# Decoder block on one core: the first two phases merged, half of a later weight product moved into them, and expert rows scattered to a table by token and choice

## What is computed

```python
mod = jax.nn.silu(c) @ w_ada[l] + b_ada[l]                       # 1024 x 6144 weights, one row of 6144
sh_m, sc_m, gt_m, sh_f, sc_f, gt_f = jnp.split(mod, 6, axis=-1)
h = modulate(rmsnorm(x, g_norm_mix[l]), sh_m, sc_m)              # needs the first 2048 columns of mod
z = h @ w_in[l]                                                  # RWKV columns, latent (MLA) columns, gates
...                                                              # RWKV scan, group norm, attention, branches
x = x + gt_m[:, None, :] * (merged @ w_out[l])
h2 = modulate(rmsnorm(x, g_norm_ffn[l]), sh_f, sc_f)             # needs columns 3072 to 5120 of mod
x = x + gt_f[:, None, :] * hier_moe(h2, ...)                     # 32 experts, 2 of them for each token
```

## Time and profile before

| | us |
|---|---|
| median of 3 runs | 1671.89 |
| lowest and highest of them | 1671.5, 1673.9 |
| profiled execution, device time | 1669.98 |
| its span | 1668.2 |
| PE busy in the span | 1427.4 (86%) |
| DMA engines busy, queue q1 (issued by SP) | 35.4% |

### The profile page before, as it was taken

The page is one execution under the profiler, slowest core; times in us unless marked ns, Lnnn a source line. Parts: engine busy times, 40 slices in busy tenths (PEclk is TensorE's granted clock), DMA queues, the critical chain, the costliest instruction groups (busy, mean ns, idle before and its releaser), DMA issues. The chain is left out here.

```text
span 1668.2 us, 32819 instructions
## 1 busy us (share of the span) xinstructions
PE 1427.4 (86%) x14321; PEld 1024.3 (61%) x14321; DVE 704.3 (42%) x991; ACT 464.2 (28%) x827; POOL 249.0 (15%) x292
## 2 busy tenths in 40 slices
PE   7499999847999984499988999999896699999980
PEld 3497777627999981277767888787785333333320
DVE  1545677566666636144444111355335221111114
ACT  0543223252434322144434222212111111111110
POOL 0001122105656520011110000000000100000003
PEclk9699999978999997699998999999997699999995
DMA  6711222100000009990002111314106789999957
GB/s 256 251 56 51 83 81 83 58 15 2 5 4 4 4 8 318 313 371 1 1 1 76 50 50 50 139 51 152 42 39 260 265 326 420 421 421 401 410 212 302
DMA packets 76582, 252.35 MB, mean 151 GB/s; under 512 B 7128, under 2 KB 32216, under 8 KB 59680
## 3 DMA queue, kind: packets, MB, share of 16 engines
q1 hardware_dynamic: 66800, 220.48, 35.4%
q0 software_dynamic: 6048, 16.79, 2.8%
q10 hardware_dynamic: 3600, 13.11, 1.9%
HBM read 211.00 MB, written 44.58 MB: 153 GB/s over the span
## 5 line engine op out<-in xcount | busy, mean ns | idle before, releaser
L2418 PE MATMUL ps<-gu,xT 128*32 128x512 f32 x1536 | 178.3, 606 | 4.6 <-DMA gu<-w_e_up 3.9
L394 PE MATMUL ps<-hs,wh 128*128 128x512 f32 x320 | 126.7, 396 | 11.5 <-DVE hs L390 7.9
L396 PE MATMUL ps<-hs,wl 128*128 128x512 f32 x320 | 126.5, 395 | 0.0
L2418 PEld LDWEIGHTS ps<-gu,xT 128*32 128x32 f32 x1536 | 48.2, 112 | 111.6 <-issue 107.6
L2640 DVE TENSOR_TENSOR sg<-sg,ps 128x256 f32<-128x256 f32 x25 | 10.5, 422 | 217.3 <-ACT sg L2504 217.3
L395 PE MATMUL ps<-hs,wh 128*128 128x512 f32 x256 | 100.6, 393 | 0.0
L390 DVE TENSOR_TENSOR wl<-wraw,wh 128x1024 fp32r<-128x1024 f32 x24 | 29.4, 1225 | 156.2 <-ACT wh L387 156.2
L394 PE MATMUL ps<-hh,wr_h 128*128 128x512 f32 x224 | 93.1, 416 | 0.6 <-DVE wr_l L390 0.6
L395 PE MATMUL ps<-hl,wr_h 128*128 128x512 f32 x224 | 88.4, 395 | 0.0
L396 PE MATMUL ps<-hh,wr_l 128*128 128x512 f32 x224 | 88.4, 395 | 0.0
L1895 DVE TENSOR_REDUCE nmax<-ps 128x1 f32<-128x896 f32 (+4 forms) x64 | 45.9, 754 | 99.9 <-PE ps L1804 99.4
(11 more groups left out here) (358 smaller groups left out, 3037.0 us busy)
## 6 DMA issues: line engine op xcount, KB each, us to landing
gu<-w_e_gate SPq DMA_DIRECT2D x34, 1024.0 KB, 13.8
gu<-w_e_up SPq DMA_DIRECT2D x34, 1024.0 KB, 16.3
dn<-w_e_down SPq DMA_DIRECT2D x34, 1024.0 KB, 12.6
wada<-w_ada SPq DMA_DIRECT2D x16, 1024.0 KB, 6.7
expert_rows<-YTM ACTq DMA_DIRECT2D x25, 512.0 KB, 8.8
wbuf<-w_ada SPq DMA_DIRECT2D x4, 2048.0 KB, 15.5
wraw<-w_gates SPq DMA_DIRECT2D x16, 512.0 KB, 3.4
expert_rows<-zrow SPq DMA_DIRECT2D x4, 2048.0 KB, 24.6
```

What stands on the lines that cost most here:

```text
L394: nc.tensor.matmul(out, wt[0], mov[0], start=(k == 0), stop=False)
L396: return nc.tensor.matmul(out, wt[1], mov[0], start=False, stop=(k == kn - 1))
L2418: last = nc.tensor.matmul(ps[part, GB[b]], xT[:, b, k, part], gu[:, expert(m, c_) % WB, :, k], start=(k == 0), stop=(k == KD - 1))
```

## The change

1. **Front.** Phase 0 is gone; its work is in phase 1. The first 2048 columns are now a `Rows` object too (`rows0`): 8 pieces of 1 MB in 8 slots, with the tiles of x loaded between them, products in four column groups. DVE adds the bias and the gain in a layout of 4 x 32 partitions, and four products with a selection matrix (`sel`) bring the rows to all 128 partitions; ACT copies `SH_M` and DVE `SC_M` out of PSUM.
2. **`rows4` moved to the front** as 16 half pieces (256 of each 512 columns, 512 KB, in runs of 1 KB) in three slots. PE makes two half pieces after the transposes of each tile. Its row is stored at the end of the front's list. `wm_l` is now made by POOL.
3. **Phase 4** keeps `rows2` alone, with 6 slots; SP issues `pair(0)` first and the other pairs right behind the pieces.
4. **Expert rows.** The table `expert_rows` has 2048 rows, one for each choice and token. POOL scatters the result rows there by indirect DMA (indices `home`), five passes behind its fetches; rows without a token are left out. The zeros are no longer written. In the last phase SP loads 16 tiles of 128 rows with plain DMAs.

```diff
+            def load(self, sp, i):
+                if i >= self.room:
+                    sp.wait_ge(self.mm, i - self.room + 1)
+                at = slice(i // KD * self.width, (i // KD + 1) * self.width)
...
+                    for k in range(KD):
+                        rows0.load(sp, k)
+                        if k % 2:
+                            load_x(k // 2)
...
+                    for t in range(NT):
+                        if t + 4 < NT:
+                            sp.wait_ge(h_ready, t + 1)
+                            load_x(t + 4)
+                        for i in range(NW + 2 * t, min(NW + 2 * t + 2, rows4.pieces)):
+                            rows4.load(sp, i)
+                        if t:
+                            store(t - 1)
...
+                    pool.wait_ge(wm_hi, 1)
+                    nc.gpsimd.tensor_tensor(wm_l[:], wm[:], wm_h[:].bitcast(f32), ALU.subtract).then_inc(wm_lo, 1)
...
-                            if t == 1:
-                                dve.wait_ge(wm_hi, 1)
-                                low_part(wm_l[:], wm[:], wm_h[:]).then_inc(wm_lo, 1)
...
+                    roots(0)
+                    rows0.add_bias(dve, CH + 2)
+                    dve.wait_ge(rows0.done, 1)
+                    nc.vector.scalar_tensor_tensor(row0[64:P], row0[64:P], 1.0, gains[64:P], ALU.add, ALU.mult)\
+                      .then_inc(rows0.done, 1)
+                    dve.wait_ge(bc_mm, 1)
+                    link(nc.vector.tensor_copy(SC_M, ps[:, 2:4].rearrange("p a n -> p (a n)")))
...
+                    for j in range(CH):
+                        m = nc.tensor.matmul(ps[:, j], sel[:, j], row0, start=True, stop=True)
+                    m.then_inc(bc_mm, 1)
...
+                        for i in range(2 * t, 2 * t + 2):
+                            rows4.products(pe, i)
                         if t >= 2:
                             mla(t - 2)
...
+                    pair(0)
                     for k in range(KD):
                         rows2.load(sp, k)
-                    pair(0)
-                    for k in range(KD):
-                        rows4.load(sp, k)
-                    rows2.store(sp, 1)
+                    for p in range(1, HEADS // 2):
+                        pair(p)
...
-                    rows4.store(sp, 2)
-                    for p in range(1, HEADS // 2):
-                        pair(p)
+                    rows2.store(sp, 1)
...
-                            sp.dma_start(free[a_], zrow[:].unsqueeze(1).broadcast_to([P, 4, D])).then_inc(z_out, 16)
...
+                    if m >= XSLOTS + 2:
+                        j = m - XSLOTS - 2
+                        pool.wait_ge(y_ev, 2 * j + 2)
+                        send(home[:, j:j + 1], j % YSLOTS)
...
-                V.tensor_scalar(idx[:], ps[:, IDX, 0:NPASS + 2], -1.0, None, ALU.add).then_inc(idx_s, 1)
+                link(V.tensor_scalar(homef[:, 0], ps[:, IDX, 0:NPASS + 2], -1.0, None, ALU.add))
+                link(V.tensor_scalar(homef[:, 1], homef[:, 0], SEQ - 0.5, -float(SEQ), ALU.is_ge, ALU.mult))
+                V.tensor_tensor(idx[:], homef[:, 0], homef[:, 1], ALU.add).then_inc(idx_s, 1)
+                V.tensor_copy(home[:], homef[:, 0]).then_inc(home_s, 1)
...
-                            pool.indirect_dma_start(
-                                out=rows[:, 2 * t + i], out_offset=None, in_=y_dram,
+                            sp.dma_start(rows[:, 2 * t + i], y_dram[at:at + P]).then_inc(r_in[2 * t + i], 16)
```

More of the change, by code:

```diff
@@ L418, in build @@
             rot = alias("rot", [P, 2, 2, QK, 16], f32)
-            with ExitStack() as scratch:
-                ang = sb(scratch, "ang", [P, NT, 16])
-                turns = sb(scratch, "turns", [P, NT, 16])
+            arows = alias("arows", [P, 3, 512], f32)
+            row0, row4, gains = (arows[:, i] for i in range(3))
             sqk = sb(st, "sqk", [P, QK, QKD])
+            c_in, c_sig, rep_s, const_in, pc_in, sel_s, bc_mm, sh_ev = sems(
+                st, "c_in", "c_sig", "arep", "const_in", "pc_in", "sel_s", "bc_mm", "sh_ev")
+            rows0 = Rows(st, 0, 6, row0, wbuf0, crep, rep_s)
+            rows4 = Rows(st, 4 * D, 7, row4, wbuf4, crep, rep_s)
             x_in = slots(st, "x_in", 4)
@@ L468, in _, with load_x @@
-                    for t in range(NT - 4, NT):
-                        store(t)
+                    def load_x(t):
+                        sp.dma_start(xt[:, t % 4], x_v[t]).then_inc(x_in[t % 4], 16)
+                    sp.dma_start(ccol[:], c[0].rearrange("(p k) -> p k", k=KD)).then_inc(c_in, 16)
+                    sp.dma_start(cst[:], consts).then_inc(const_in, 16)
+                    rows0.load_bias(sp)
+                    for j in range(2):
+                        half = slice(j * 512, (j + 1) * 512)
+                        sp.dma_start(gains[QUARTERS[2 + j]], g_norm_mix[:, half].broadcast_to([32, 512]))\
+                          .then_inc(rows0.b_in, 16)
@@ new lines, in _ @@
+                    for k in range(KD):
+                        rows0.load(sp, k)
+                        if k % 2:
+                            load_x(k // 2)
+                    sp.dma_start(wm[:], w_mla).then_inc(wm_in, 16)
+                    rows4.load_bias(sp)
+                    for j in range(2):
+                        half = slice(j * 512, (j + 1) * 512)
+                        sp.dma_start(gains[QUARTERS[j]], g_norm_ffn[:, half].broadcast_to([32, 512]))\
+                          .then_inc(rows4.b_in, 16)
@@ new lines, in _ @@
+                    for i in range(NW):
+                        rows4.load(sp, i)
+                    for b in range(2):
+                        sp.dma_start(wr[:, b], w_rwkv[b]).then_inc(wr_in[b], 16)
+                    sp.dma_start(pc[:], pcol).then_inc(pc_in, 16)
+                    sp.dma_start(posi[:], pos).then_inc(m_in, 16)
+                    sp.dma_start(g_row[:].rearrange("p a n -> p (a n)"),
+                                 qk_gain.broadcast_to([P, 2 * QKD])).then_inc(m_in, 16)
@@ L470, in _ @@
+                    store(NT - 1)
+                    rows4.store(sp, 2)
                     for b in range(2):
@@ L650, in tile_low, with roots @@
                         low_part(hl[:, :, cols], stage[:, t % 2], hh[:, :, cols]).then_inc(h_lo, 1)
-                    for half in range(2):
+                    def roots(half):
                         cols = slice(4 * half, 4 * half + 4)
@@ L790, in mla @@
                         m.then_inc(mla_mm, 1)
+                    for k in range(KD):
+                        rows0.products(pe, k)
+                    pe.wait_ge(rows0.done, 2)
+                    pe.wait_ge(sel_s, 1)
+                    for j in range(CH):
+                        m = nc.tensor.matmul(ps[:, j], sel[:, j], row0, start=True, stop=True)
+                    m.then_inc(bc_mm, 1)
                     for t in range(NT):
@@ L1595, in _ @@
                     rows2.load_bias(sp)
-                    rows4.load_bias(sp)
-                    for j in range(2):
-                        sp.dma_start(gffn[QUARTERS[j]], g_norm_ffn[:, j * 512:(j + 1) * 512].broadcast_to([32, 512]))\
-                          .then_inc(rows4.b_in, 16)
                     def pair(p):
@@ L1688, in _ @@
                 def _(pe):
-                    def row_products(i):
-                        (rows2, rows4)[i // KD].products(pe, i % KD)
                     pe.wait_ge(wg_in, 16)
-                    for i in range(EARLY):
-                        row_products(i)
                     for t in range(NT):
@@ L1706, in _ @@
                         m.then_inc(gm, 1)
-                        row_products(EARLY + t)
-                    for i in range(EARLY + NT, 2 * KD):
-                        row_products(i)
+                        rows2.products(pe, t)
         zst.close()
@@ L2692, in _ @@
                 def _(sp):
+                    for t in range(NT):
+                        for i in range(2):
+                            at = i * SEQ + t * P
+                            sp.dma_start(rows[:, 2 * t + i], y_dram[at:at + P]).then_inc(r_in[2 * t + i], 16)
                     for t in range(NT):
```

222 lines of the change are left out of this document (91 added, 131 removed).

## The result

| | median, us | profiled span, us | ratio to before |
|---|---|---|---|
| before | 1672.33 | 1668.2 | |
| after | 1647.1 | 1640.4 | 0.9846 (95% interval 0.9817 to 0.9876) |

Predicted were 1645.1 us (1633 to 1658). The changed kernel's executions lie further apart than those of the kernel before: 1642.19 to 1650.92 against 1671.5 to 1673.9. The profiled one is the shortest of four, so its difference in span (27.8 us) is larger than the difference of the medians (25.2). In a second set of five it came to 1642.45 us, 0.9842 (0.9821 to 0.9864).

The account below looks back on a forecast made before the run. PE was taken to bound phase 0 and the expert passes, DMA phase 4. Terms 0 - 1.5 + 26 - 0.4 + 2.7 = 26.8 us, off the 1671.89 us median, gave 1645.1 us, range 1633 to 1658.

Parts of the forecast that it names:

- Front, 0: Start to the end of mla(7): no net gain, mla(7) ending at 113.9 us as before; between +5 and -10.
- Half pieces: Front, from mla(0) to mla(7): ten half pieces of rows4 on PE at 0.53 us each add 5.3 us.
- Clears, -1.5: Semaphore clears: 21 more at up to 0.10 us each, a loss of 0 to 2.1 us, taken as 1.5.
- Phase 4, +26: Phase 4: attention starts at 679.3 instead of 705.34 us, a gain of 26 us, between +33 and +19.
- rival B: Phase 4: compute ends last and SP is never held, +33 us there, 1638 us in all; chance 0.15.
- Experts, 0: Expert passes: PE's missing 4 us could come back at best; no gain was taken for the passes.
- rival D: Expert passes: the scatter's writes are dear and the kernel is slower than before, 1693 us at 100 GB/s; chance 0.03.
- Handover and last phase, +2.7: End of kernel: last phase starts 0.9 us later but ends at 1665.5, a gain of 2.7 us, between +6 and -1.
- A: Front: with three slots for rows4, PE waits for half pieces; five rounds cost 10 us, 1655 us in all; chance 0.12.
- C: Attention: PE waits for pair(1) while loads still move, 10 us of phase 4's gain lost, 1655 us; chance 0.05.

Follow-up runs that it names:

- rows4_back: Changed kernel with rows4 loaded and multiplied in phase 4 again, merged front and scatter kept: 1660.49 us, 0.9940 of before.
- late_pairs: Changed kernel with the loads of pairs 2 and 3 issued first thing in attention's phase instead of in phase 4: 1635.7 us, 0.9789 of before.
- wml_early: Changed kernel with wm_h made on ACT before its copy of the spread rows and wm_l on DVE before its copy: 1645.51 us, 0.9831 of before.

## Why the prediction held, point by point

**Front, 0.** Right in sum (1.1 us gained at the last latent copy), by two errors against each other and one size. The first scaled tile was put at 46.8 and came at 44.22. The spreading products took 5.21 us, as put. POOL had to do 1.06 us for `g_row`, not the 3.50 of the earlier trace rows (those began 0.43 us behind DVE's `wm_l` and ended 0.31 behind its end: most of them was a hold too), and began `wm_l` at 48.35 instead of 52.9. `mla(0)` was put at 64.9 and came at 63.67, but not by the mechanism named. I had read the earlier trace rows as two engines that slow each other, and scaled both by columns: 12.0 us for POOL. What happens is a hold: POOL ran at 2.39 ns a column (7.95 us for 3328), no slower than the 2.53 that I had taken for POOL alone, and DVE stood still until it was done. The Trainium skill says so on a page that I had not drawn on (SBUF — State Buffer, section "Who interferes with whom"): a DVE instruction with two SBUF inputs contends with a POOL instruction that reads SBUF, and the ports that the two share go to whichever issues first for its whole instruction; the other is blocked, not throttled. The trace agrees: 7.78 us for an operation of 1.22, ended 1.1 us behind POOL's. The later rows show the same when POOL's two operations, which stand in one row there, are taken one by one. The second of them, and DVE's next operation:

```profile
310.10 2.83 POOL L514 TENSOR_TENSOR qk<-qk,g_row 128x768 f32<-128x768 f32 x1
311.14 2.87 DVE L390 TENSOR_TENSOR wr_l<-wr,wr_h 128x1024 fp32r<-128x1024 f32 x1
```

POOL's first one ended at 310.14 and DVE's 2.76 us at 311.22; POOL's second ended at 312.93 and DVE's 2.87 at 314.01. Each DVE operation ended 1.1 us behind a POOL operation, as in the changed kernel. They took turns.

**Half pieces.** 0.53 us each was right (two take 1.07 us at full clock). rows4_back shows that rows4 costs the front 4.0 us, where the sum had 5.3 less 3.5 for a wait that was to go. That the wait would go because x's tiles no longer queue behind the weights was wrong: 1.64 us of it are still there, and without the half pieces it is 2.49 as before.

**Clears, -1.5.** From DVE's last shift to its first operation of the next phase were 4.64 us and are 6.26, 1.6 more for 25 more clears, so 0.06 each; at the end of phase 4 clears and meeting took 2.16 us. Right.

**Phase 4, +26; 21.8 measured.** The pairs were out at 670.65 (671 put) and computation ended at 667.75 (668 to 672 put). The step that failed is one term: the two stores of `yT`, put at 5 us between bounds of 1 and 12, took 9.97. These 5.0 us alone turn the 679.3 put into 684.3, and 684.40 was measured. (In the table's stretch the loss is 4 us, since the phase itself began 0.9 us later than before.) That SP's queue is what is late next was right, and late_pairs shows it: without pairs 2 and 3 ahead of the stores the phase ends with its computation, and +33 (rival B) becomes real.

**Experts, 0; 5.4 measured.** The upper bound was named ("PE's missing 4 us could come back at best") and 0 was taken for it. The row that should have decided was in rival D itself: 8.4 MB of scatter for 13.1 MB of stores in passes whose DMA engines are full. That this was used only for the risk, and not for the forecast, was the mistake. The bound was too low as well: 2.9 us of PE's waits for weights came back, and its busy time became 2.8 us shorter, which no term of the prediction had.

**Handover and last phase, +2.7; 0.5 measured.** The phase itself is 3.1 shorter (3.6 put). The handover is 2.6 longer instead of 0.9: POOL starts the scatter 0.7 later behind DVE than ACT did its store, its issue takes 0.64 longer, and the rest of 1.3 us lies between issue and the first load of the next phase (landing, meeting, clears).

**Rivals.** A: its waits exist (1.9 us of PE for half pieces) but something longer covers them; they decide in wml_early. C: no wait of the scores for a pair. D: nothing of it, the share of POOL's queue is 2.7% as against 2.8%.

## What to carry over

When a phase ends with the queue that issues the DMAs, look first at what it issues for later phases: six loads moved over the boundary gave 9 us by the ratios in the kernel after, nine loads 10.7 in the kernel before, for under 1 us in attention. If fewer bytes go through full DMA engines, put the gain into the forecast: at least what PE waits for those engines, here 4 us of which 2.9 came back, with 5.4 gained in all. Be slow to put a long operation with two SBUF inputs on POOL while DVE has such operations on the critical path, even if DVE is the busier one: here it held DVE for 6.6 us (7.78 less 1.22) to save it 3.62.

A phase that ends earlier is not yet a gain: follow it over the next boundary. Here 2 us of the front were lost in the next phase to a granted clock of 0.63 and 0.81 instead of 1.00.

## What was not expected of the hardware

- Between POOL and DVE there is no sharing on a two-input operation: 7.95 us unhindered on one side, 7.78 instead of 1.22 on the other, and DVE's end 1.1 us behind POOL's in every case looked at.
- Two stores of 1 MB behind short-run loads held SP's queue for 9.97 us, while a single load of a pair held it for up to 9.24; SP then can't issue the small stores behind them.
- The granted clock between 340 and 358 us differed in two kernels whose instructions there are the same: 0.62, 1.00, 1.00 for a start at 336.05 and 0.66, 0.63, 0.81 for one at 334.17.
